# Scan of the state space: sums of the way back in TensorE's accumulation, one subtraction on GpSimd

## What is computed

```
dt = exp(log_dt);  mag = exp(lam_re*dt);  ab = mag*(cos(lam_im*dt) + i*sin(lam_im*dt))
bu_re, bu_im = u @ bb_re, u @ bb_im          # 64 groups of 16 channels, 64 complex states each
s[t] = ab*s[t-1] + bu[t]                     # over 256 positions, complex
y = s_re @ c_re - s_im @ c_im                # back to 16 channels a group
y = y + d*xin;  g = gelu(y);  out = g*sigmoid(g @ w_glu + b_glu)
```

## Time and profile before

| | us |
|---|---|
| median of 3 runs | 3323.88 |
| lowest, highest | 3319.11, 3325.11 |
| profiled execution, its time | 3326.23 |
| profiled execution, its span | 3324.4 |
| TensorE busy | 3202.7 (96%) |
| VectorE busy | 1854.0 (56%) |
| ScalarE busy | 1390.6 (42%) |
| GpSimd busy | 211.3 (6%) |

### The profile page before, as it was taken

One profiled execution on the slowest core, in us unless ns is written; L12 is line 12 of the kernel. 1 busy time (PEld: TensorE's weight loads), 2 busy tenths in 40 slices (PEclk: granted clock), 3 DMA queues, 4 the chain that ended last, 5 costly groups with the idle time before them and its releaser, 6 DMA issues.

```text
span 3324.4 us, 46398 instructions
## 1 busy us (share of the span) xinstructions
PE 3202.7 (96%) x18890; PEld 2765.0 (83%) x18890; DVE 1854.0 (56%) x2392; ACT 1390.6 (42%) x1943; POOL 211.3 (6%) x263
## 2 busy tenths in 40 slices
PE   8999999998899999999998999999999999999998
PEld 7777777766777777878797778999998989889896
DVE  3333333366567777777656884444565555545454
ACT  2222222244455656656541013665434434434343
POOL 0000000020000000000138640000000000000000
PEclk9999999999999999999998998999999999999999
DMA  6222222222257778878553333444554555545454
GB/s 239 81 77 81 84 76 86 80 76 79 105 225 293 302 276 319 319 275 306 214 190 125 116 115 133 152 165 179 215 190 178 203 190 189 187 175 190 183 184 149
DMA packets 81787, 581.72 MB, mean 175 GB/s; under 512 B 9010, under 2 KB 9266, under 8 KB 12339
## 3 DMA queue, kind: packets, MB, share of 16 engines
q1 hardware_dynamic: 78912, 566.27, 46.5%
q10 hardware_dynamic: 2674, 12.54, 1.0%
HBM read 574.58 MB, written 4.19 MB: 174 GB/s over the span
## 4 chain that ended last, share of the span: by engine, by line
PE 81%; DVE 10%; DMA 3%; ACT 2%; POOL 2%; issue 1%; SPq 0%; ACTq 0%; DVEq 0%; POOLq 0%
PE PG L721 10%; PE PG L661 8%; PE PG L659 8%; PE PG L662 8%; PE PG L686 5%; PE PG L687 5%; PE PG L685 5%; PE PG L1030 4%; PE PG L1031 3%; PE PG L1032 3%; PE PX L791 3%; DMA ring<-weights 3%; DVE work L2224 2%; PE PG L630 1%; PE PX L1071 1%
## 5 line engine op out<-in xcount | busy, mean ns | idle before, releaser
L549 DVE TENSOR_TENSOR ring_r<-ring,work_r 128x1024 fp32r<-128x1024 f32 x532 | 630.4, 1226 | 386.8 <-ACT work_r L542 380.4
L542 ACT ACTIVATE work_r<-ring 128x1024 fp32r<-128x1024 f32 x532 | 534.5, 1053 | 562.7 <-PE PG L662 234.3
L721 PE MATMUL PG<-HT,ring 128*128 128x256 f32 x1728 | 436.9, 391 | 0.0
L549 DVE TENSOR_TENSOR ring_r<-ring,C_r 128x1024 fp32r<-128x1024 f32 x244 | 289.2, 1226 | 223.1 <-ACT C_r L542 219.7
L542 ACT ACTIVATE C_r<-ring 128x1024 fp32r<-128x1024 f32 x244 | 244.9, 1052 | 381.6 <-PE PG L662 262.3
L662 PE MATMUL PG<-work_r,ring_r 128*128 128x256 f32 x1344 | 375.2, 279 | 3.4 <-issue 3.4
L662 PE MATMUL PG<-YT_r,ring_r 128*128 128x256 f32 x1280 | 361.4, 282 | 0.0
L721 PEld LDWEIGHTS PG<-HT,ring 128*128 128x128 f32 x1728 | 312.7, 191 | 55.7 <-issue 10.6
L662 PEld LDWEIGHTS PG<-work_r,ring_r 128*128 128x128 f32 x1344 | 254.7, 190 | 3.8 <-issue 3.8
L686 PE MATMUL PG<-ring_r,HT_r 128*128 128x512 f32 x640 | 252.4, 394 | 0.0
L662 PEld LDWEIGHTS PG<-YT_r,ring_r 128*128 128x128 f32 x1280 | 244.8, 191 | 0.0
(11 more groups left out here) (541 smaller groups left out, 6375.3 us busy)
## 6 DMA issues: line engine op xcount, KB each, us to landing
ring<-weights SPq DMA_DIRECT2D x536, 1024.0 KB, 4.8
XT<-xT SPq DMA_DIRECT2D x4, 512.0 KB, 6.1
XT<-x ACTq DMA_DIRECT2D x1, 2048.0 KB, 9.5
residual<-XT ACTq DMA_DIRECT2D x4, 512.0 KB, 3.1
XT<-residual ACTq DMA_DIRECT2D x1, 2048.0 KB, 11.6
result<-YT SPq DMA_DIRECT2D x8, 256.0 KB, 4.1
C<-constants ACTq DMA_DIRECT2D x1, 1608.0 KB, 9.0
work<-gate_up ACTq DMA_DIRECT2D x1, 1024.0 KB, 13.3
```

Of the source, the lines that this page charges most:

```text
L542: act.activation(w_high(u)[:, c], ring[:, u % RING, c], ACT.Copy).then_inc(w_hi, 1)
L549: dve.tensor_tensor(ring_r[:, u % RING, c], ring[:, u % RING, c], w_high(u)[:, c].bitcast(F32), ALU.subtract).then_inc(w_lo, 1)
L721: mm = pe.matmul(PG[:, u % BANKS, 0:T], ring[:, u % RING, k * P:k * P + P], HT[:, k, :], start=(k == 0), stop=(k == KT - 1))
```

## The change

The two sums of the way back are no longer made on VectorE. It leaves four products, `s_re*cos` and `-s_im*sin` in the two halves of `TR`, `s_re*sin` and `s_im*cos` in the two halves of `XR`, and TensorE sums all four in PSUM: 16 output products a block in place of 8, the first two with `CD[:, 0]`, the last two with `CD[:, 1]`. The sign goes into one instruction with two tiles and a constant (`scalar_tensor_tensor`). The subtraction of the way in, which makes the imaginary input, moves to GpSimd: VectorE makes its two products first and raises `c_x`, GpSimd subtracts and raises `c_sub`, and VectorE scans the real part before it waits for `c_sub` and scans the imaginary part. On GpSimd the subtraction of block `b` stands between the table of block `b` and that of block `b + 1`.

```diff
-        c_pow = sem("s5_powers")
+        c_sub = sem("s5_imaginary_inputs")
...
                 for i in range(4):
-                    for c in range(2):
-                        s = (TR[:, 0, :], XR[:, 1, :])[c]
+                    for n, (c, s) in enumerate(((0, TR[:, 0, :]), (0, TR[:, 1, :]), (1, XR[:, 0, :]), (1, XR[:, 1, :]))):
                         mm = pe.matmul(PX[32 * i:32 * i + 32, 0, 0:T], CD[:, c, 4 * b + i, :], s[:, i * T:i * T + T],
-                                       start=(c == 0), stop=(c == 1))
+                                       start=(n == 0), stop=(n == 3))
                 mm.then_inc(c_y, 1)
...
+                tt(x1, bu(1), er, ALU.mult)
+                tt(t1, bu(0), ei, ALU.mult).then_inc(c_x, 1)
                 tt(x0, bu(0), er, ALU.mult)
-                tt(t0, bu(1), ei, ALU.mult)
-                tt(x1, bu(1), er, ALU.mult)
-                link(tt(t1, bu(0), ei, ALU.mult))
-                tt(x0, x0, t0, ALU.add)
-                tt(x1, x1, t1, ALU.subtract).then_inc(c_x, 1)
-                dve.wait_ge(c_x, b + 1)
-                for i in range(4):
-                    mag = S_MAG[:, 4 * b + i:4 * b + i + 1].to_broadcast([P, T])
-                    for x in (x0, x1):
+                link(tt(t0, bu(1), ei, ALU.mult))
+                link(tt(x0, x0, t0, ALU.add))
+                for x in (x0, x1):
+                    if x is x1:
+                        dve.wait_ge(c_sub, b + 1)
+                    for i in range(4):
+                        mag = S_MAG[:, 4 * b + i:4 * b + i + 1].to_broadcast([P, T])
                         ins = dve.tensor_tensor_scan(x[:, i, :], mag, x[:, i, :], 0.0, ALU.mult, ALU.add)
                 link(ins)
                 tt(t0, x0, er, ALU.mult)
-                link(tt(t1, x1, ei, ALU.mult))
-                link(tt(t0, t0, t1, ALU.subtract))
-                tt(t1, x0, ei, ALU.mult)
-                link(tt(x1, x1, er, ALU.mult))
-                tt(x1, x1, t1, ALU.add).then_inc(c_s, 1)
+                dve.scalar_tensor_tensor(t1, x1, -1.0, ei, ALU.mult, ALU.mult)
+                tt(x0, x0, ei, ALU.mult)
+                tt(x1, x1, er, ALU.mult).then_inc(c_s, 1)
...
                     else:
                         ins.then_inc(c_tab, 1)
+                pool.wait_ge(c_x, b + 1)
+                tt(XR[:, 1, :], XR[:, 1, :], TR[:, 1, :], ALU.subtract).then_inc(c_sub, 1)
```

## The result

The changed kernel takes 3326.76 us (median of 22 runs, 3320.63 to 3330.17), the kernel before in the same comparison 3321.95 (22 runs). The ratio is 1.0014, 95% interval 1.0008 to 1.0021: slower by 4.8 us, where 6.5 us faster was forecast, and 1.3 us above the stated range.

What follows compares the result with a forecast made beforehand. VectorE was taken to pace the scan blocks, with GpSimd's table binding after the change. Block 0 -3.0, blocks 1 to 6 -1.7, block 7 -1.4, clock -0.4 gave -6.5 us: 3323.88 to 3317.4 us, range 3312.5 to 3325.5.

Steps and rivals of the forecast that it cites:

- (c): TensorE's output products per block: 32 records for 16 add 0.87 us, bounds 0 to +6.1.
- block 0 to 1: First block of the scan: 21.6+4.77+1.7 = 28.1 us until block 1 starts, against 31.1, so -3.0.
- the table's 26.86: Blocks 1 to 6: GpSimd's next table sets the start-to-start time, 26.86 us against 27.14, together -1.7 us.
- the third: Output products between states and addition do not spread over column groups: slower, 3328 or 3357 us; chance 0.12.
- the milder form: Output products with two column groups at once: +2.6 us, cycle 27.2 to 28.1, total 3328; chance 0.08.
- the end of the stretch: Block 7 to L659, with no table behind it: TensorE's units end it, -1.4 us.
- the clock: TensorE waits less before L659 and may keep its clock: 0 to -1.5 us, -0.4 taken.
- the turns of GpSimd and VectorE: SBUF work in each block: short GpSimd steps alternate with 1024-wide VectorE operations every 1.56 us, both paying.
- the first bound: Back product with two tiles and a constant takes turns with GpSimd like the others; otherwise states come 0.4 us earlier.
- Rivals 1 and 2: GpSimd's table: quicker and not binding, 3312.1 us, chance 0.10; or longer, cycle 27.8, 3323.5 us, chance 0.17.
- the sign: Block-to-block cycle under 26.4 us, or TensorE's inputs as releaser, would speak for the table not binding.
- rival 1: GpSimd's table does not bind; outputs to inputs set the pace, 25.9 us a block, 3312.1 us; chance 0.10.

Runs made afterwards that it cites:

- e1: Changed kernel with its 16 output products reordered, product as outer loop and column group as inner; 3313.19 us, ratio 0.9973 to the kernel before.
- e4: Changed kernel with the subtraction back on VectorE and output products spread, column group as inner loop; 3303.47 us, ratio 0.9942 to the kernel before.
- e8: Changed kernel with the subtraction back on VectorE, output products still in runs per column group; 3323.98 us, ratio 1.0003 to the kernel before.
- e7: Kernel before with only the subtraction moved to GpSimd, way back and eight output products as before; 3330.88 us, ratio 1.0019 to the kernel before.
- e6: Kernel before with each output product made twice, in runs of four per column group, nothing else; 3331.38 us, ratio 1.0024 to the kernel before.

## Why the prediction was wrong

**The step that failed** is the term of the output products in (c), "Doubled: +0.87 us if four column groups still run side by side [...] I take 0.87, since the rows of the same line are nearest". It measured 3.50 at full clock (4.59 against 1.09) and 5.3 in block 0 (7.30 against 1.96). The mechanism that I had seen, four groups at once, exists, but it has a condition that the rows of before could not show, since all their runs were four records long: with runs of four records it holds, with runs of six and eight only in part. I read a pace off a pattern and kept the pace while changing the pattern. Put 3.50 and 5.3 into the prediction's own sum: block 0 to 1 21.6+4.77+5.3 = 31.7 (30.8 measured, the clock came back during the products), the blocks 21.6+3.50+2.99 = 28.1 (28.02), and the change is slower. The path named with it failed too: 28.1 is above the table's 26.86, so the blocks wait for the states and the output products, not for GpSimd's table as the prediction had it.

**The rival that came true** is the third, with a chance of 0.12. It had the place and the sign right; its prices for the products were +2.6 us (two groups at once) or +6.1 (one), and the measured +3.50 lies between: a group's run of eight records lasts 1.9 us and the next group's starts after 0.9, so two groups go at once for part of the time. The time, 3326.8, is 1 us under the milder form's 3328, since block 0 and the end cost less than the 5 us put down for them.

The Trainium skill (TensorE: Matmul & The Clock Gate, Part 3: Packing small matmuls) lets matmuls start and end only in program order. It pointed to the side that came true. An estimate by it, with 0.216 us between records of one group and none between groups: 32 records in runs of eight would take some 6.4 us, 16 in runs of four some 3.0, and 32 spread ones 1.9. The runs have 4.59, 1.09 and 1.93, so only the spread order agrees. The measurements decide for a limit per column group, not for strict order.

**Right, as e1 shows**, in which only (c) is put back to what the prediction assumed: outputs 1.93 us (1.96), block 1 28.11 after block 0 (28.1), blocks 26.85 apart (26.86). The table released five of the seven starts. Block 7 to L659 took 23.1 (23.9), since the inputs of block 7 were ready earlier than I took. Together e1 has -6.9 us in the stretch (212.4 against 219.25) where -6.1 were forecast, and 9 us in all (5.6 to 12 by the interval) where it was 6.5. What lies beyond the stretch in it is the clock behind L659 (-1.4, bound 0 to -1.5, of which I had taken 0.4); the rest is not resolved. So with outputs of 1.93 us the forecast would have been near, and its two smallest terms, the end of the stretch and the clock, were each taken some 0.8 to 1.0 us too small.

**Right in the changed kernel as well:** the turns of GpSimd and VectorE, to 0.05 us; the instruction with two tiles and a constant (L2226) takes its turns, 1.64 us beside GpSimd and 1.22 alone in e4. So the first bound held. The Trainium skill (SBUF — State Buffer, Who interferes with whom) says that any VectorE instruction with two SBUF inputs contends with a GpSimd one that reads SBUF, and this trace agrees (1.64 against 1.22). **Rivals 1 and 2** did not occur: GpSimd did not get in more quickly (the table is ready after 26.74 us, the sign was under 26.4) nor later (27.8). That the table does not bind in the changed kernel has another reason than rival 1's, the longer outputs. The stated range, 3312.5 to 3325.5, also left rival 1's own 3312.1 just outside, though the text says that it holds it.

**The two halves of the change** are now apart. The way back in TensorE's sums is worth 19 us when its products are spread (e4) and nothing when they stand in runs (e8). The subtraction on GpSimd costs: 6 us alone (e7), 0.8 us a block in runs (28.02 against 27.19, e8), 2.3 a block in the spread order (26.87 against 24.61 in the mean, e1 and e4). In runs this 0.8 is TensorE's wait for the states (0.76 us a block), which e8 does not have.

**Open:** where the limit of four records sits, in a queue of each column group or in TensorE's issue, was not separated, nor whether it counts records, products (each leaves two records here) or the weight load that goes with each. Runs of five records were not tried, and only 128 x 32 weights with 256 float32 columns.

## What to carry to other kernels

When small products go to column groups of TensorE, try the column group as the inner loop: here two loops exchanged took the same 16 products from 4.59 to 1.93 us and the kernel from even to 19 us faster. A duration that was measured side by side holds for its own order and run length only; when a change lengthens the run, bound it by the serial price and look for what decides between the two. Work given to an engine with spare time lands in that engine's order: ask what queues behind it, and from when on the queued work will now collide with its neighbour.

## What was not expected of the hardware

- Column groups ran side by side with runs of four records, two float32 products; with runs of six and eight the next group started with the fourth record from the end of the run before it (1.09, 2.87 and 4.59 us for runs of 4, 6 and 8).
- The wait before L659 fell from 2.89 to 1.80 us and the clock stayed at its upper level (granted 1.00, 2.4 GHz, in place of 0.50; a first product of 0.36 us, not 0.55). That gave 1.4 us behind L659, on top of the 1.1 of the shorter wait.
- Work added to TensorE was partly repaid elsewhere: with outputs 3.5 us longer and nothing else changed (e6), blocks grew by 0.9 us in the mean. The states came 2.0 us earlier, as GpSimd's table moved into the gap, and the clock no longer fell (0.7).
